# Quarter buffers at the in-projection's and the keys' operands; first quarters of each MLP loaded during the projection before it

## The chip, the cores and the metric

One Trainium2 chip, one core. The metric is the device time of one execution in microseconds (us); the kernel before was run three times, and the median counts. One further execution was taken by the hardware profiler, and all rows shown here come from it.

## The reference, cut to what matters

Batch 1, 512 tokens, width 1024, two layers, float32 throughout. Shown as code; `mlp` runs twice, once in each layer.

```python
def sq_relu_mlp(h, w1, w2):                 # w1 1024x4096, w2 4096x1024
    u = relu(h @ w1)
    return (u * u) @ w2

# layer 0: recurrent block
xb, yb = split(rmsnorm(x) @ w_in + b_in)            # in-projection, 1024x2048
hs = rg_lru(conv4(xb));  x = x + (hs * gelu(yb)) @ w_out   # out-projection, 1024x1024
x = x + sq_relu_mlp(rmsnorm(x), w1[0], w2[0])
k, v = split(rmsnorm(x) @ w_kv)
# layer 1: differential attention on k, v, 8 heads
x = x + diff_attention(rmsnorm(x) @ w_q, k, v) @ w_o       # attention's output projection
x = x + sq_relu_mlp(rmsnorm(x), w1[1], w2[1])
return rmsnorm(x)
```

## The kernel before, in words

Weights lie in memory as tiles of 128 x 1024 floats (512 KB) and are used in a fixed order. Each float32 tile is split into a high and a low part: ScalarE (ACT) copies it to `w_hi` (line 618), VectorE (DVE) subtracts to get `w_lo` (line 1120), and TensorE (PE) multiplies three times (hi by hi, hi by lo, lo by hi). `w_hi` and `w_lo` have four slots each, so the split of tile t waits until PE has done tile t-4. In the program's code "tile 20" is the fifth tile of the layer-0 out-projection: tiles 0 to 15 are the in-projection, 16 to 23 the out-projection, 24 to 51 the first of four groups of layer 0's MLP.

The MLP uses a seven-product scheme (Strassen's) on halves: each group of 1024 hidden units has seven products up and seven down, with two tiles of 24 matmuls for each product. Some products need sums of quarters of the weights. Those are built in two buffers, `q1` and `q2` (two tiles each). A plain load by the SyncE (SP) queue brings a quarter (A21, line 453), and GpSimd (POOL) issues an accumulating DMA that adds another quarter from memory onto it (line 547). A third step is an addition on DVE, `quarter_sum` (line 1452). The seven up products use, in order: A11 (ring), q2 = A21+A22, q2 plus A11 added by DVE, A12 (ring), q1 = A21+A11, q2 plus A12 added by DMA, A22 (ring).

Tiles that need no sum go through a ring of two raw buffers, `w_raw`, loaded by SP (line 442). Ring load r waits until the tile that used the buffer before is split. The two loads of A12 have one more condition: they wait for `quarter_sum`, since that reads A11 out of the ring buffers.

SP, ACT, DVE and POOL each run one program in order. For the first group of an MLP, SP's order is: all ring loads of the projection before; the two halves of q2; the two halves of q1; A11; A12; and on. These q loads wait for a semaphore that says the old data under the buffers is dead (`olo_done` for layer 0, `scores_mm` for layer 1). POOL's order is: `add_first` (A22 onto q2), the accumulation of the squares for the norm (`accumulate`, lines 535), then `add_others`, which begins with A11 onto q1.

`residual_step` runs on ACT and DVE beside the last projection tiles: for each of eight row blocks m it adds the projection to x, splits the weight tile four ahead, and builds the MLP's operands `x_raw`, `x_sum`, `x_hi`, `x_lo`. After it DVE does `quarter_sum` twice. In the first group, ACT and DVE then split tiles 4, 5, 6, 7 of the group (6 and 7 are A12), and only behind tile 7 compute the norm (`norm_guess`, `norm_newton`; its first DVE step is line 1170). PE starts the fourth up product only when the norm's sums have been copied out of a bank that this product uses (`sums_copied`). In layer 1 PE also transposes x between the first four products (`turn_x`, line 2001, eight blocks a pair); ACT empties the banks (`turned_rows`, line 905), in its program also behind the split of tile 7.

SBUF is shared over time: a region is used by the recurrent block, then by MLP 0; the attention uses the same addresses, then MLP 1. Before, `x_hi` and `x_lo` (28 KB a partition each) lie at the start and q1, q2 (8 KB each) behind them, over `lru_v` and `lru_x` in layer 0 and over `u_lo` and `kq` in layer 1. `in_hi` and `h_hi` are the first 16 KB.

Of the kernel before, what the change touches and what calls it, by code (L numbers as in the profile page):

```python
# [8 lines left out]
P = 128  # L9
D = 1024  # L10
S = 512
NCH = D // P
HEADS = 8
# [6 lines left out]
TILE = NCH * P  # L20
QB = S // P
# [14 lines left out]
T_OUT = len(IN_ORDER)  # L36
# [41 lines left out]
T_O = T_QK + 2 * HEADS  # L78
# [12 lines left out]
R_MLP0 = T_MLP0  # L91
R_V = R_MLP0 + R_PER * GROUPS
R_MLP1 = R_V + T_MLP1 - T_V
# [9 lines left out]
def up_tile(layer, g, p):  # L103
    return (T_MLP0, T_MLP1)[layer] + PER * g + p


def down_tile(layer, g, p):
    return up_tile(layer, g, 2 * NPROD + p)
# [19 lines left out]
A11, A12, A21, A22, B12, B11, B22, B21 = range(0, 16, 2)  # L128
# [4 lines left out]
def stored_tile(layer, g, place):  # L133
    return W_MLP[layer] + W_PER * g + place
# [7 lines left out]
O_M0 = O_Y + NCH  # L142
# [34 lines left out]
RING = 4  # L177
WARM_UP = 2
RAWS = 2
# [6 lines left out]
def build(nc, x_t, weights, gate_weights, vectors, lam_vecs, final_gain, out):  # L186
    F32 = mybir.dt.float32
# [5 lines left out]
    with keep:  # L193
        def sb(name, shape, dt, stack=keep):
            return stack.enter_context(nc.sbuf_tensor(name, shape, dt))

        def sem(name):
            return keep.enter_context(nc.semaphore(name))
# [7 lines left out]
        region = ExitStack()  # L206
# [12 lines left out]
        out_lo = sb("out_lo", [P, NCH, S], F32R, region)  # L219
        region.close()  # L220

        region = ExitStack()
        gain_rows = sb("gain_rows", [P, D], F32, region)
        region.close()

        region = ExitStack()
        x_hi = sb("x_hi", [P, NOP, PAIRS, HALF], F32R, region)
        x_lo = sb("x_lo", [P, NOP, PAIRS, HALF], F32R, region)
        q1 = sb("q1", [P, 2, TILE], F32, region)
        q2 = sb("q2", [P, 2, TILE], F32, region)  # L230
        first = ExitStack()
        x_raw0 = sb("x_raw0", [P, NCH, 2, HALF], F32, first)
        x_sum0 = sb("x_sum0", [P, 3, 4, HALF], F32, first)
# [69 lines left out]
        tile_done = sem("tile_done")  # L303
# [3 lines left out]
        olo_done = sem("olo_done")  # L307
# [34 lines left out]
        scores_mm = sem("scores_mm")  # L342
# [61 lines left out]
        def quarter_loads(layer, g, n):  # L404
            return 16 * (2 * (layer * GROUPS + g) + n + 1)
# [4 lines left out]
        def quarter_adds(layer, g, n, half):  # L410

            return 4 * (layer * GROUPS + g) + 2 * n + half + 1
# [8 lines left out]
        @block.sync  # L421
        def _(sp):
            def load_half(t, n):
                ks = slice(n * TILE // 2, (n + 1) * TILE // 2)
                sp.dma_start(w_raw[:, t, ks], weights[t][:, ks]).then_inc(half_in[2 * t + n], 16)

            def load_x(m):
                sp.dma_start(x[:, m, :], x_t[m]).then_inc(x_in[m], 16)


            load_x(0)
            load_half(0, 0)
            load_half(1, 0)
            load_x(1)
            load_half(0, 1)
            load_half(1, 1)
            for m in range(2, NCH):
                load_x(m)
            def load_ring(r, tile):

                sp.wait_ge(wlo_done, RING_TILES[r - RAWS] + 1)
                sp.dma_start(w_raw[:, r % RAWS, :], weights[tile]).then_inc(raw_in[r % RAWS], 16)

            def load_quarter(layer, g, q, place, free):

                for half in range(2):
                    if free is not None:
                        sp.wait_ge(wlo_done, free + half + 1)
                    elif layer:
                        sp.wait_ge(scores_mm, QB * HEADS)  # L450
                    else:
                        sp.wait_ge(olo_done, O_M0)
                    sp.dma_start(QUARTERS[q][:, half, :],
                                 weights[stored_tile(layer, g, place + half)]).then_inc(quarter_in[q][half], 16)

            def load_group(layer, g):
                r = (R_MLP0, R_MLP1)[layer] + R_PER * g

                def two(r, place):
                    for half in range(2):  # L460
                        load_ring(r + half, stored_tile(layer, g, place + half))

                load_quarter(layer, g, "q2", A21, down_tile(layer, g - 1, 8) if g else None)
                if g:
                    two(r, A11)
                    load_quarter(layer, g, "q1", A21, down_tile(layer, g - 1, 12))
                else:
                    load_quarter(layer, g, "q1", A21, None)
                    two(r, A11)
                for half in range(2):  # L470

                    sp.wait_ge(quarter_added, quarter_adds(layer, g, 0, half))
                    load_ring(r + 2 + half, stored_tile(layer, g, A12 + half))
                two(r + 4, A22)
                load_quarter(layer, g, "q1", B11, up_tile(layer, g, 8))
                load_quarter(layer, g, "q2", B12, up_tile(layer, g, 10))
                two(r + 6, B22)
                two(r + 8, B21)

            for r in range(RAWS, R_MLP0):  # L480
                load_ring(r, r)
            for g in range(GROUPS):
                load_group(0, g)
            for r in range(R_V, R_MLP1):
                load_ring(r, W_MLP[1] - R_MLP1 + r)
            for g in range(GROUPS):
                load_group(1, g)


            sp.wait_ge(tile_done, down_tile(1, GROUPS - 1, 0))  # L490
            sp.dma_start(gain_rows[:, :], final_gain).then_inc(gain_in, 16)

            for n, tok in enumerate((0, 1, 2, 3)):
                for half, done in ((1, out_act), (0, out_dve)):
                    sp.wait_ge(done, n + 1)
                    sp.dma_start(out[tok][:, HALVES[half]], y[:, tok, HALVES[half]]).then_inc(stored, 16)
            sp.wait_ge(stored, 16 * QB * 2)
# [3 lines left out]
        def _(pool):  # L501
# [36 lines left out]
            def add_quarter(layer, g, q, place, split=None, loaded=None, added=None):  # L538

                for half in range(2):  # L540
                    if loaded is not None:
                        pool.wait_ge(quarter_in[q][half], quarter_loads(layer, g, loaded))
                    if split is not None:
                        pool.wait_ge(wlo_done, split + half + 1)
                    if added is not None:
                        pool.wait_ge(quarter_added, quarter_adds(layer, g, added, half))
                    nc.gpsimd.dma_start(QUARTERS[q][:, half, :], weights[stored_tile(layer, g, place + half)],  # L547
                                        accum_op=ALU.add).then_inc(sum_in[q][half], 16)

            def add_first(layer, g):  # L550
                add_quarter(layer, g, "q2", A22, loaded=0)

            def add_others(layer, g):
                add_quarter(layer, g, "q1", A11, loaded=0)
                add_quarter(layer, g, "q2", A12, split=up_tile(layer, g, 4))
                add_quarter(layer, g, "q1", B22, split=down_tile(layer, g, 2))
                add_quarter(layer, g, "q2", B22, loaded=1, added=1)
                add_quarter(layer, g, "q1", B21, split=down_tile(layer, g, 4))

            add_first(0, 0)  # L560
            accumulate(N_M0, 0)
            def constants():
# [12 lines left out]
                                        ALU.add).then_inc(consts_done, 1)  # L575

            add_others(0, 0)
            constants()
            for g in range(1, GROUPS):
                add_first(0, g)  # L580
                add_others(0, g)

            add_first(1, 0)
            accumulate(N_M1, 1)
            add_others(1, 0)
            for g in range(1, GROUPS):
                add_first(1, g)
# [519 lines left out]
        def _(dve):  # L1107
            own = Own(dve, dve_own)

            def split_lo(t):  # L1110
                if t >= TILES:
                    return
                quarter = quarter_of(t)
                if quarter is None:
                    src = w_raw[:, RING_OF[t] % RAWS, :]
                else:
                    _, _, (q, _, _, _), half = quarter
                    src = QUARTERS[q][:, half, :]
                dve.wait_ge(whi_done, t + 1)
                nc.vector.tensor_tensor(w_lo[:, t % RING, :], src, w_hi[:, t % RING, :],  # L1120
                                        ALU.subtract).then_inc(wlo_done, 1)
# [1210 lines left out]
```

## Time and profile before

| | us |
|---|---|
| three runs | 1055.74, 1056.50, 1056.93 |
| median | 1056.5 |
| profiled execution, its own time | 1058.89 |
| its span in the profile | 1057.1 |
| PE busy in the span | 1035.2 (98%) |
| DVE busy | 813.7 (77%) |
| ACT busy | 644.7 (61%) |
| mean granted TensorE clock | 0.994 |

Busy times are of one engine each; they run beside each other. The span is from the first to the last instruction that the profile shows. A granted clock of 1.00 is 2.4 GHz and 0.50 is 1.2 GHz.

### The profile page before, as it was taken

Reading aid. Unit: us, or ns where it says so; the run is one execution under the profiler, and the core shown is the slowest. Engines: PE = TensorE matmul, PEld = TensorE weight load, DVE = VectorE, ACT = ScalarE, POOL = GpSimd, SP = SyncE. Lnnn points to the kernel's source line nnn. Section 1 sums busy time; section 2 is a strip of 40 time slices with the busy share of each in tenths; the row PEclk is TensorE's granted clock in tenths of the full one; section 3 lists DMA queues with packets and bytes.
Section 4 is the critical chain, followed back from the end, with each engine's and each line's share of the span. In section 5 each row is a group of like instructions: output and inputs, shape, how many; then the busy total and the mean of one; then the engine's idle time right before and its main releaser. Section 6 shows DMA issues by size and latency. Waiting matters only on the chain.

```text
span 1057.1 us, 15296 instructions
## 1 busy us (share of the span) xinstructions
PE 1035.2 (98%) x5920; PEld 885.5 (84%) x5920; DVE 813.7 (77%) x1157; ACT 644.7 (61%) x940; POOL 108.2 (10%) x133
## 2 busy tenths in 40 slices
PE   8999999999999999999999999999899999999995
PEld 6777889979989989988877777779888988988984
DVE  6988875886896896898656666566598698698697
ACT  7698864745745745665336656566664664664665
POOL 1000021121111101100000000012011011011012
PEclk9999999999999999999999999999999999999998
DMA  7222288498498498462321111167779678779672
GB/s 253 91 81 80 81 229 211 117 252 231 115 256 228 118 258 230 115 173 88 112 63 58 60 60 41 60 187 145 207 143 246 209 151 244 203 152 252 193 156 104
DMA packets 47592, 165.29 MB, mean 156 GB/s; under 512 B 5408, under 2 KB 5536, under 8 KB 47392
## 3 DMA queue, kind: packets, MB, share of 16 engines
q1 hardware_dynamic: 31536, 109.59, 30.2%
q0 software_dynamic: 15552, 53.48, 27.7%
q10 hardware_dynamic: 432, 1.24, 0.3%
q8 instruction: 47, 0.77, 0.3%
q14 instruction: 25, 0.20, 0.1%
HBM read 159.05 MB, written 2.10 MB: 152 GB/s over the span
## 4 chain that ended last, share of the span: by engine, by line
PE 87%; DVE 5%; DMA 5%; ACT 1%; issue 1%; SPq 0%; DVEq 0%; ACTq 0%
PE ps L1982 27%; PE ps L2017 27%; PE ps L1849 21%; DMA w_raw<-weights 5%; PE ps L2080 4%; PE ps L2139 2%; PE ps L2165 2%; DVE w_lo L1120 1%; PE ps L1908 1%; PE ps L2154 1%; DVE value L1499 1%; ACT w_hi L618 1%; DVE acc L1149 0%; DVE q L1452 0%; DVE x_lo L1401 0%
## 5 line engine op out<-in xcount | busy, mean ns | idle before, releaser
L1982 PE MATMUL ps<-x_hi,w_hi 128*128 128x256 f32 x896 | 255.2, 285 | 3.3 <-DVE cols L1170 2.0
L1982 PE MATMUL ps<-x_lo,w_hi 128*128 128x256 f32 x896 | 254.4, 284 | 0.0
L1982 PE MATMUL ps<-x_hi,w_lo 128*128 128x256 f32 x896 | 254.3, 284 | 0.0
L618 ACT ACTIVATE w_hi<-w_raw 128x1024 fp32r<-128x1024 f32 x134 | 140.5, 1055 | 170.2 <-DMA w_raw<-weights 127.8
L1120 DVE TENSOR_TENSOR w_lo<-w_raw,w_hi 128x1024 fp32r<-128x1024 f32 x134 | 163.9, 1224 | 89.4 <-ACT w_hi L618 88.9
L1120 DVE TENSOR_TENSOR w_lo<-q,w_hi 128x1024 fp32r<-128x1024 f32 x144 | 176.3, 1227 | 42.9 <-ACT w_hi L618 42.0
L618 ACT ACTIVATE w_hi<-q 128x1024 fp32r<-128x1024 f32 x144 | 150.9, 1052 | 93.4 <-PE ps L1982 42.1
L2017 PE MATMUL ps<-w_hi,a_hi 128*128 128x512 f32 x448 | 176.2, 393 | 1.8 <-DVE w_lo L1120 1.2
L1982 PEld LDWEIGHTS ps<-x_hi,w_hi 128*128 128x128 f32 x896 | 172.9, 193 | 4.1 <-DVE cols L1170 2.2
L2017 PE MATMUL ps<-w_hi,a_lo 128*128 128x512 f32 x448 | 174.6, 390 | 0.0
L2017 PE MATMUL ps<-w_lo,a_hi 128*128 128x512 f32 x448 | 174.5, 390 | 0.0
L547 POOL DMA_DIRECT2D q<-weights x96 | 83.5, 965 | 882.7 <-DMA q<-weights 515.8
L1982 PEld LDWEIGHTS ps<-x_lo,w_hi 128*128 128x128 f32 x896 | 173.0, 193 | 0.3
L1982 PEld LDWEIGHTS ps<-x_hi,w_lo 128*128 128x128 f32 x896 | 172.9, 193 | 0.0
L2017 PEld LDWEIGHTS ps<-w_hi,a_hi 128*128 128x128 f32 x448 | 84.1, 188 | 25.1 <-issue 4.6
L2017 PEld LDWEIGHTS ps<-w_lo,a_hi 128*128 128x128 f32 x448 | 84.1, 188 | 17.9
L2017 PEld LDWEIGHTS ps<-w_hi,a_lo 128*128 128x128 f32 x448 | 84.2, 188 | 16.3
L1499 DVE SCALAR_TENSOR_TENSOR value<-ps,scale,value 128x512 f32<-128x512 f32 x104 | 73.0, 742 | 3.2 <-PE ps L2017 2.8
L1849 PE MATMUL ps<-in_hi,w_hi 128*128 128x512 f32 x128 | 54.3, 424 | 1.8 <-DVE in_lo L1125 0.8
L1849 PE MATMUL ps<-in_lo,w_hi 128*128 128x512 f32 x128 | 50.5, 395 | 0.0
L1849 PE MATMUL ps<-in_hi,w_lo 128*128 128x512 f32 x128 | 50.4, 394 | 0.0
L976 ACT ACTIVATE prob_t<-ps 128x512 f32<-128x512 f32 (+3 forms) x32 | 14.1, 441 | 44.1 <-PE ps L2165 23.7
(218 smaller groups left out, 1666.8 us busy)
## 6 DMA issues: line engine op xcount, KB each, us to landing
w_raw<-weights SPq DMA_DIRECT2D x134, 512.0 KB, 4.4
q<-weights POOLq DMA_DIRECT2D x96, 512.0 KB, 8.1
q<-weights SPq DMA_DIRECT2D x64, 512.0 KB, 4.6
x<-x_t SPq DMA_DIRECT2D x8, 256.0 KB, 6.6
y_t<-value SPq DMA_DIRECT2D x8, 256.0 KB, 2.3
acc<-work POOLq DMA_DIRECT2D x6, 256.0 KB, 3.3
rstd<-work POOLq DMA_DIRECT2D x6, 256.0 KB, 3.5
w_raw<-weights SPq DMA_DIRECT2D x4, 256.0 KB, 4.7
```

The costliest lines, as they stand in the source:

```text
L547: nc.gpsimd.dma_start(QUARTERS[q][:, half, :], weights[stored_tile(layer, g, place + half)], accum_op=ALU.add).then_inc(sum_in[q][half], 16)
L618: nc.scalar.activation(w_hi[:, t % RING, :], src, ACT.Copy).then_inc(whi_done, 1)
L976: nc.scalar.activation(prob_t[:, j % 2, 0:n], ps[:, BANK_T, 0:n], ACT.Copy).then_inc(trans_read, 1)
L1120: nc.vector.tensor_tensor(w_lo[:, t % RING, :], src, w_hi[:, t % RING, :], ALU.subtract).then_inc(wlo_done, 1)
L1499: return nc.vector.scalar_tensor_tensor(out=to, in0=bank, scalar=scale2[:, half, tok:tok + 1], in1=to, op0=ALU.mult, op1=ALU.add)
L1849: ins = nc.tensor.matmul(ps[:, bank, :], w[:, slot, ws], o[:, k, :], start=(k == 0 and n == 0), stop=(k == NCH - 1 and n == 2))
L1908: ins = nc.tensor.matmul(ps[:, bank, :], gw[:, ws], lru_v[:, m, :], start=True, stop=True)
L1982: ins = nc.tensor.matmul(to, w[:, t % RING, ws], o[:, op, j, :], start=fresh and j == 0 and f % 2 == 0 and n == 0, stop=j == PAIRS - 1 and ...
L2017: ins = nc.tensor.matmul(ps[:, bank, :], a[:, a_slot, j, ts], w[:, slot, ws], start=first and a is a_hi and w is w_hi, stop=end and w is w ...
L2080: ins = nc.tensor.matmul(ps[:, 4 * half + tok, :], o[:, k, ts], w[:, t % RING, cs], start=(i == 0 and n == 0), stop=(i == NCH - 1 and n == 2))
L2139: ins = nc.tensor.matmul(ps[:, BANK_SCORES + 2 * (j % 2) + c, 0:n], kq[rows, h % 2, 1, qb * P:(qb + 1) * P], kq[rows, h % 2, 0, 0:n], star ...
L2165: ins = nc.tensor.matmul(ps[:, BANK_O, qb * P:(qb + 1) * P], prob_t[:, j % 2, kb * P:(kb + 1) * P], value[:, kb, h * P:(h + 1) * P], start ...
```

## The change

The two quarter buffers move to the first 16 KB of the region, that is over `in_hi` (in-projection operand) and over `h_hi` (the keys' operand); `x_hi` and `x_lo` move 16 KB up. Their first loads wait for the end of the in-projection (`tile_done` 16) and of the last key tile (`tile_done` T_O). On SP these four loads move ahead of three ring loads in layer 0's out-projection (right behind ring load 20) and ahead of two ring loads in layer 1's output projection (behind ring load R_MLP1-3). On POOL the addition of A11 onto q1 moves from `add_others` to `add_first`, ahead of the accumulation of squares. Groups 1 to 3 keep their orders.

```diff
+        q1 = sb("q1", [P, 2, TILE], F32, region)
+        q2 = sb("q2", [P, 2, TILE], F32, region)
+        final = ExitStack()
+        gain_rows = sb("gain_rows", [P, D], F32, final)
+        final.close()
         x_hi = sb("x_hi", [P, NOP, PAIRS, HALF], F32R, region)
         x_lo = sb("x_lo", [P, NOP, PAIRS, HALF], F32R, region)
-        q1 = sb("q1", [P, 2, TILE], F32, region)
-        q2 = sb("q2", [P, 2, TILE], F32, region)
...
                     if free is not None:
                         sp.wait_ge(wlo_done, free + half + 1)
-                    elif layer:
-                        sp.wait_ge(scores_mm, QB * HEADS)
                     else:
-                        sp.wait_ge(olo_done, O_M0)
+                        sp.wait_ge(tile_done, (T_OUT, T_O)[layer])
...
-                load_quarter(layer, g, "q2", A21, down_tile(layer, g - 1, 8) if g else None)
                 if g:
-                    two(r, A11)
+                    load_quarter(layer, g, "q2", A21, down_tile(layer, g - 1, 8))
+                two(r, A11)
+                if g:
                     load_quarter(layer, g, "q1", A21, down_tile(layer, g - 1, 12))
-                else:
-                    load_quarter(layer, g, "q1", A21, None)
-                    two(r, A11)
...
+            def first_quarters(layer):
+                load_quarter(layer, 0, "q2", A21, None)
+                load_quarter(layer, 0, "q1", A21, None)
+
             for r in range(RAWS, R_MLP0):
                 load_ring(r, r)
+                if r == R_MLP0 - RING:
+                    first_quarters(0)
...
             for r in range(R_V, R_MLP1):
                 load_ring(r, W_MLP[1] - R_MLP1 + r)
+                if r == R_MLP1 - RAWS - 1:
+                    first_quarters(1)
...
             def add_first(layer, g):
                 add_quarter(layer, g, "q2", A22, loaded=0)
+                add_quarter(layer, g, "q1", A11, loaded=0)
 
             def add_others(layer, g):
-                add_quarter(layer, g, "q1", A11, loaded=0)
```

## Rows read from the trace of the kernel before

**Rows 1.** Waits of PE over the whole span: us in total, times, longest.
```profile
PE ps L2001 <- ACT value L905: 3.2, 1, 3.2
PE ps L1982 <- DVE cols L1170: 2.0, 1, 2.0
PE ps L1982 <- DVE x_lo L1401: 1.3, 1, 1.3
```
**Rows 2.** Stretches; after the engines' busy us come granted clock, DMA share, GB/s.
```profile
177.00:178.00 1.00, 1.00 (x6) 1.00 (x6) 0.99 (x3) 1.00 (x2) 0.00 (x0) 0.50 1.03 274
...
724.00:726.00 2.00, 2.00 (x18) 2.00 (x19) 1.21 (x3) 1.48 (x3) 0.67 (x1) 1.00 0.43 76
...
744.00:745.00 1.00, 0.80 (x4) 0.80 (x5) 0.86 (x4) 1.00 (x3) 0.00 (x0) 0.50 1.02 270
```
**Rows 3.** The chain that ended last, in order of time: start, us, what.
```profile
163.18 10.73 DMA w_raw<-weights
...
176.37 24.79 PE ps L1982 x192
...
397.66 40.31 PE ps L1982 x336
...
731.63 10.56 DMA w_raw<-weights
...
752.32 0.87 PE ps L2001 x8
753.19 17.27 PE ps L1982 x144
```
**Rows 4.** PE in order of time: where stages begin, and before the longest gap.
```profile
111.59 0.39 PE L1849 MATMUL ps<-out_hi,w_hi 128*128 128x512 f32 x1
...
155.11 0.28 PE L1982 MATMUL ps<-x_hi,w_hi 128*128 128x256 f32 x1
...
718.14 0.28 PE L1982 MATMUL ps<-x_hi,w_hi 128*128 128x256 f32 x1
...
740.71 0.28 PE L1982 MATMUL ps<-x_hi,w_lo 128*128 128x256 f32 x1
```
**Rows 5.** POOL, ACT and DVE in order of time, 160 to 176 us.
```profile
160.68 2.12 POOL L547 DMA_DIRECT2D q<-weights  x2
...
173.93 1.06 ACT L618 ACTIVATE w_hi<-w_raw 128x1024 fp32r<-128x1024 f32 x1 [2.93 <-DMA w_raw<-weights]
...
175.02 1.22 DVE L1120 TENSOR_TENSOR w_lo<-w_raw,w_hi 128x1024 fp32r<-128x1024 f32 x1 [3.68 <-ACT w_hi L618]
```
**Rows 6.** The page's queues (packets, MB, share of 16 engines), q1 SP's, q0 POOL's.
```profile
q1 hardware_dynamic: 31536, 109.59, 30.2%
q0 software_dynamic: 15552, 53.48, 27.7%
```
**Rows 7.** From issue to landing, DMAs of `w_raw`, then of `q`.
```profile
DMA to landing us min/median/max: 3.2/4.4/10.7
DMA to landing us min/median/max: 3.4/6.9/13.3
```
**Rows 8.** SP's issues of the first quarters, layer 0 and layer 1.
```profile
131.39 1.88 SPq L453 DMA_DIRECT2D q<-weights  x4
...
699.12 1.86 SPq L453 DMA_DIRECT2D q<-weights  x4
```
**Rows 9.** DVE: splits of tile 18, of tile 21, and of layer 1's tile T_O+3.
```profile
109.45 1.22 DVE L1120 TENSOR_TENSOR w_lo<-w_raw,w_hi 128x1024 fp32r<-128x1024 f32 x1
...
129.76 1.23 DVE L1120 TENSOR_TENSOR w_lo<-w_raw,w_hi 128x1024 fp32r<-128x1024 f32 x1
...
679.38 1.22 DVE L1120 TENSOR_TENSOR w_lo<-w_raw,w_hi 128x1024 fp32r<-128x1024 f32 x1
```
**Rows 10.** Stretches of four us, columns as in rows 2.
```profile
120.00:124.00 4.00, 4.00 (x19) 3.34 (x18) 3.04 (x5) 2.31 (x4) 0.00 (x0) 1.00 0.00 2
...
684.00:688.00 4.00, 4.00 (x23) 3.34 (x22) 0.65 (x4) 2.06 (x13) 0.00 (x0) 1.00 0.01 4
```

More of the change, by code:

```diff
@@ L222, in build @@
         region = ExitStack()
-        gain_rows = sb("gain_rows", [P, D], F32, region)
-        region.close()
-        region = ExitStack()
+        q1 = sb("q1", [P, 2, TILE], F32, region)
[3 more added lines that the diff above has]
+        final.close()
         x_hi = sb("x_hi", [P, NOP, PAIRS, HALF], F32R, region)
         x_lo = sb("x_lo", [P, NOP, PAIRS, HALF], F32R, region)
-        q1 = sb("q1", [P, 2, TILE], F32, region)
-        q2 = sb("q2", [P, 2, TILE], F32, region)
         first = ExitStack()
```

## The prediction

> **What bounds the kernel now.** I read the table of busy times first: PE is busy 1035.2 of 1057.1 us, so only PE's gaps, and stretches in which its clock is low, can be won by moving transfers. Then PE's waits, to see which gaps there are. Three of the largest lie where an MLP begins: 2.0 us before the fourth up product of layer 0, and in layer 1 1.3 and 3.2 us [rows 1]. The windows then show the clock: 0.50 at 177 us and at 744 us, after each of the two longer gaps, but 1.00 after the gap of 1.3 us [rows 2]. Last the chain, to see what made the gaps: in both layers it runs through one ring load, the second half of A12, that takes 10.7 and 10.6 us [rows 3], where the median of all ring loads is 4.4 [rows 7].
>
> The named releasers are not the cause. In layer 0 the wait is put down to the norm's first step on DVE, but by program order that step stands behind the split of tile 7 (A12's second half), which ACT begins at 173.93 after 2.9 us of waiting for the DMA, and DVE ends at 176.24 [rows 5]. In layer 1 the emptying of the transposes' banks stands behind the same split. The DMA is slow because of company: POOL has put two accumulating transfers (A11 onto q1) in flight at 160.68 [rows 5], and two more follow.
>
> **What the gaps cost in all.** A 256-column matmul costs 40.31/336 = 0.120 us in steady state [rows 3].
> - Layer 0: PE restarts at 176.37 after 2.05 idle, so it was free at 174.3. The 192 matmuls from there take 24.79 where 192 x 0.120 = 23.04 would do [rows 3]: 1.75 us of half clock. Together 3.8 us.
> - Layer 1, long gap: PE is free at 740.71 + 0.28 = 740.99 [rows 4], and the fifth product starts at 753.19 [rows 3]. Between lie two groups of eight transposes (0.87 us each [rows 3]) and 48 matmuls (5.76): 7.5 us of work in 12.2 us. Loss 4.7 us.
> - Layer 1, short gap: 1.3 us [rows 1].
>
> Sum 9.8 us: that is the most this change can take out of these places.
>
> **The change part by part.**
>
> *Loads of the first quarters earlier.* Four loads a layer. Nothing is added; queue shares give their price: SP's queue moves 109.59 MB in 30.2% of 1057.1 us, so 512 KB (0.524 MB) occupy all 16 engines for 1.53 us; POOL's accumulating queue 53.48 MB in 27.7%, so one accumulating transfer 2.87 us [rows 6]. Layer 0: ring load 20 is issued when tile 18 is split (110.7 [rows 9]); the wait for the in-projection ends at about 111.6 to 112, when out_hi matmuls have begun [rows 4]. The loads then go out some 19.5 us before their present 131.4 [rows 8]. Layer 1: ring load T_O+5 goes out when T_O+3 is split, 680.6 [rows 9]; the last key tile was done before, so the wait is met, and the loads are issued at 681 instead of 699.1 [rows 8]. Both stretches have idle DMA: share 0.00 at 120 to 124 and 0.01 at 684 to 688 [rows 10].
>
> *Both additions right behind them.* 4 x 1.53 + 4 x 2.87 = 17.6 us of DMA a layer. Layer 0: from 112, over by about 131 if little else is served. Layer 1: 681 to 699, so it is out of the way when the last splits begin. POOL has nothing ahead of these issues that is pending and nothing behind that is due earlier (the squares come from ACT at about 135), so its queue loses nothing. Issue costs (0.47 us on SP, about 0.9 on POOL) lie on idle queues.
>
> *The new wait on SP.* Behind it are ring loads 21 to 23, of which 21 may not be issued before tile 19 is split, at 124.5. The wait ends 12 us before that: cost 0. The same in layer 1, with T_O+6 at about 696.
>
> *Ring loads delayed in layer 0.* Load 21 (124.5) now meets the rest of the additions: up to (131 - 124.5) = 6.5 us of DMA work, or none. Tile 21's split ended at 131.0 [rows 9]; PE needs it 16.32 us (three tiles of 5.44) before 155.11, at 138.8 [rows 4]. So 7.8 us of cover against at most 6.5: cost 0, or up to 1 us with no cover left. From 131 on the ring loads meet less than before.
>
> *A12 loads, layer 0.* Their issue is fixed by quarter_sum: the second at 163.18, which is 8.07 after the first up matmul at 155.11 [rows 3, 4]. Two additions less in flight are 5.7 us less of DMA work. Before, it landed at 173.9; now at 173.9 - 5.7 = 168.2. With 1.06 and 1.22 for the splits the norm starts at 170.6, against PE's need at 174.3: gap 0, 3.7 us to spare. Bounds: if the load gets none of the 5.7 us, the gap of 2.0 and the slow clock stay (3.8 us kept); if all, 0. I take 0, since the engines were saturated at that time (DMA share 1.03 right after [rows 2]).
>
> The Trainium skill ("DMA: Bandwidth & Descriptors", the anatomy of one SWDGE transfer) gives about 2.0 us plus bytes / 436 GB/s for any such transfer, so by it (an estimate) the two additions carry only 2.4 us, A12 lands at 171.5, the norm starts at 173.9 and PE still waits for nothing, with 0.4 us to spare. The queue shares of this trace give 2.87 us for each [rows 6], more than twice the rule; I go by the trace.
>
> *Layer 1.* The 1.3 us gap is x_lo of row block 6, whose DVE steps sit behind splits that waited for A11's late ring load. With q loads and additions over by 699 this load is alone with its kind (3.2 to 4.4 us [rows 7]), and the residual steps follow PE as in layer 0, where this gap does not exist: 1.3 won. Second A12 load: 718.14 + 8.07 = 726.2 instead of 731.6 [rows 3, 4]. It takes 10.56 - 5.74 = 4.8, lands at 731.0; ACT is through tile 7, the norm and the two bank copies at about 733.7. PE arrives at 740.99 - 1.3 = 739.7: gap 0, 6 us to spare, 4.7 won. If the load kept its full 10.6 us it would land at 736.8 and still be in time: layer 1's gain does not hang on the DMA's price.
>
> *Addresses.* x_hi and x_lo lie 16 KB higher. A steady up phase mixes reads of both, which lie 28 KB apart, and comes out at an even 0.120 a matmul [rows 3]; no row shows another placement. I take 0; the third digit of that mean bounds it, 0.0005 x 2688 matmuls = 1.3 us either way.
>
> *What is late next.* Tiles 8 and 9 (q1) are ready early; tiles 10 and 11 need A12 onto q2, issued at 164.8 and 166.7 as before but with less company, and PE wants them at 174.3 + 11.5 = 185.8. From there on the groups are PE-bound: the middle groups take 40.31 us up with no gap. The kernel's tail hangs on PE's end and shifts with it.
>
> Sum: 3.8 + 1.3 + 4.7 = 9.8 us. The profiled execution took 1058.89 (span 1057.1); 9.8 less gives 1049.1 (span 1047.3). The runs' median, 1056.5, is 2.4 below the profiled one; the same difference gives **1046.7**.
>
> **The rivals.**
> 1. *Layer 0 keeps its gap in part.* For it: only 3.7 us of reserve, and load 21 to 25 now mix with additions, so DVE might reach quarter_sum later. Against: the reserve above. If nothing is won there: 1056.5 - 6.0 = 1050.5; if 0.5 us of gap stays without a drop of the clock, as after the 1.3 us gap [rows 2]: 1047.2.
> 2. *The change doesn't reach the gaps.* The norm itself is late (squares by accumulating DMA) and not the split ahead of it. For it: the named releaser. Against: PE ran its sums for the norm during the second product without waiting. Time 1056.5.
> 3. *Slower.* Place: layer 0's out-projection. The early transfers lengthen ring loads 21 to 25. Two buffers give a loop: two tiles per load time + 2.3 us for the splits, while PE uses two in 10.9, so it falls behind when a load takes over 8.6 us, and 7.8 us are in hand. At the longest landing seen, 13.3 [rows 7], 2.5 pairs lose 11.8, less 7.8, plus 1.75 for the clock: 5.7 us, time 1052.4. It decides the sign from loads of 15.0 us on; at twice the longest ring load (21.4) it costs 26 and gives 1072.7. The Trainium skill (same page, "Issuing engines are not separate DMA queues") says that transfers of all queues interleave on the same 16 engines, which is this mechanism; the slow A12 loads agree with it. Against: only 17.6 us of DMA work in all, most of it over before load 21.
>
> **How the numbers follow.** Forecast 0.74 (1045.8 to 1047.8). Rival 1: 0.18 (1047.2 to 1050.5). Rival 2: 0.03. Rival 3: 0.05, of which 0.03 ends slower. The range has the forecast and rival 1 in it, and 1.4 us below the forecast for addresses and for small DMA waits that also go: 1045.3 to 1050.5. A measurement tells 0.2% (2.1 us) from no change; faster 0.94, same 0.03, slower 0.03.
>
> **What would show it.** PE's waits for DVE cols, ACT value and DVE x_lo gone; clock 1.00 through both starts; the A12 loads at 4 to 6 us; first fourth-product matmul of layer 0 at 174.3; q additions at 113 to 131 and 682 to 699; PE busy in layer 0's out-projection. It is wrong if A12 still takes over 8 us, if PE waits in the out-projection, or if the first groups get new gaps.

## The result, and the profile after

The changed kernel takes 1047.52 us in the median of four runs (1046.32 to 1047.70), the one before 1056.55 (1055.74 to 1056.93). The ratio is 0.9913 with a 95% interval of 0.9896 to 0.9930, so 7.4 to 11.0 us less. In a later comparison with more rounds the same kernel had 1047.39 against 1057.03, ratio 0.9904 (0.9890 to 0.9918). The prediction was 1046.7 in a range of 1045.3 to 1050.5.

Two rival explanations stood against the forecast's ("company": A12's loads are slow because the two additions of A11 are in flight beside them) when the experiments began: that the new addresses make the gain ("layout"), and that the early loads do it by themselves ("earliness").

First PE's waits in the profile after (us in total, times, longest). None of the three waits of [rows 1] is left: none for the banks' copies, for the norm's first step or for x_lo.

```profile
PE ps L1919 <- POOL cols L513: 1.7, 1, 1.7
PE ps L2022 <- DVE w_lo L1125: 1.3, 1, 1.3
PE ps L1854 <- DVE w_lo L1143: 0.7, 1, 0.7
PE ps L1854 <- DVE w_lo L1125: 0.4, 1, 0.4
```

All four were there before too (1.7, 1.2, 0.7 and 0.4 us). The chain that ended last (start, us, what) shows both starts as PE alone; in [rows 3] it ran through ring loads of 10.7 and 10.6 us. The first five lines are layer 0, the rest layer 1.

```profile
99.91 54.40 PE ps L1854 x240
154.31 11.51 PE ps L1987 x96
165.82 1.68 PE ps L1897 x16
167.50 28.90 PE ps L1987 x240
196.40 8.64 PE ps L2022 x38
...
720.10 5.75 PE ps L1987 x48
725.85 1.68 PE ps L1897 x16
727.53 0.93 PE ps L2006 x8
728.46 5.75 PE ps L1987 x48
734.21 0.87 PE ps L2006 x8
735.08 5.75 PE ps L1987 x48
740.83 0.87 PE ps L2006 x8
741.71 17.27 PE ps L1987 x144
```

Windows of the profile after, columns as in [rows 2]; first one where [rows 2] had half clock, then four us of layer 1's up matmuls. PE is busy throughout at full clock, and in the first the DMA moves 90 GB/s.

```profile
177.00:178.00 1.00, 1.00 (x11) 1.00 (x9) 0.55 (x1) 0.42 (x1) 0.00 (x0) 1.00 0.74 90
...
728.00:732.00 4.00, 4.00 (x36) 4.00 (x35) 2.09 (x8) 2.85 (x6) 0.00 (x0) 1.00 1.02 215
```

The page's queues after: as many packets and bytes as in [rows 6], so the change moved transfers and took none away.

```profile
q1 hardware_dynamic: 31536, 109.59, 30.3%
q0 software_dynamic: 15552, 53.48, 28.0%
```

SP and POOL in order of time in the profile after. The four loads a layer go out at 110.8 and 676.2, where [rows 8] had 131.4 and 699.1, and all four additions follow at once.

```profile
110.82 1.77 SPq L452 DMA_DIRECT2D q<-weights  x4
...
676.17 1.86 SPq L452 DMA_DIRECT2D q<-weights  x4
```

```profile
115.73 1.03 POOL L552 DMA_DIRECT2D q<-weights  x1 [109.34 <-DMA q<-weights]
...
120.46 0.86 POOL L552 DMA_DIRECT2D q<-weights  x1 [0.47 <-DMA q<-weights]
...
680.73 0.84 POOL L552 DMA_DIRECT2D q<-weights  x1 [232.84 <-DMA q<-weights]
...
685.97 0.86 POOL L552 DMA_DIRECT2D q<-weights  x1 [1.35 <-DMA q<-weights]
```

ACT and DVE in layer 0 after: the late split of tile 21 (the price of the early transfers), and A12's second half with the norm behind it. In [rows 5] ACT began that split at 173.93, after 2.93 us of waiting for the DMA; now it begins at 166.78 and waits for nothing, for the load landed at 166.60, 4.4 us after its issue, where it had taken 10.7.

```profile
132.07 1.06 ACT L623 ACTIVATE w_hi<-w_raw 128x1024 fp32r<-128x1024 f32 x1 [4.26 <-DMA w_raw<-weights]
133.16 1.23 DVE L1125 TENSOR_TENSOR w_lo<-w_raw,w_hi 128x1024 fp32r<-128x1024 f32 x1 [4.42 <-ACT w_hi L623]
...
166.78 1.05 ACT L623 ACTIVATE w_hi<-w_raw 128x1024 fp32r<-128x1024 f32 x1
...
169.00 0.15 DVE L1175 TENSOR_SCALAR cols<-ps 128x4 f32<-128x4 f32 x1
```

Layer 1's long gap has one cause more. There A12's loads themselves went out late, since `quarter_sum` waits for A11's ring loads. The second of these took 10.5 us before (the chain, first line below); after, ACT begins the splits of both halves of A11 (the other two lines) without a wait.

```profile
705.75 10.49 DMA w_raw<-weights
```

```profile
703.63 1.04 ACT L623 ACTIVATE w_hi<-w_raw 128x1024 fp32r<-128x1024 f32 x1
...
707.08 1.04 ACT L623 ACTIVATE w_hi<-w_raw 128x1024 fp32r<-128x1024 f32 x1
```

Counted from the first up matmul of layer 1, the second load of A12 went out at 13.5 us before and at 9.7 after.

Two stretches tell the rest, and they can be read from every profile: from the first up matmul of an MLP to its first down matmul. "Start" is when PE begins layer 0's MLP, "rest" what follows layer 1's stretch. The labels are explained with the experiments.

| profile | start | layer 0 | between | layer 1 | rest | span |
|---|---|---|---|---|---|---|
| before | 155.11 | 45.89 | 517.14 | 52.16 | 286.80 | 1057.1 |
| before, second profile | 154.41 | 45.61 | 517.87 | 51.40 | 287.41 | 1056.7 |
| layout only | 154.94 | 44.10 | 517.40 | 50.05 | 287.21 | 1053.7 |
| layer 0 only | 154.09 | 42.10 | 517.14 | 50.90 | 286.07 | 1050.3 |
| layer 1 only | 154.40 | 44.01 | 517.90 | 45.49 | 287.10 | 1048.9 |
| loads early, additions late | 154.58 | 45.62 | 517.66 | 45.69 | 287.15 | 1050.7 |
| loads late, additions early | 154.75 | 42.09 | 517.63 | 53.66 | 285.07 | 1053.2 |
| plain loads for additions | 154.83 | 42.57 | 517.31 | 48.54 | 285.95 | 1049.2 |
| company put back | 154.87 | 44.10 | 517.89 | 45.50 | 285.94 | 1048.3 |
| each layer its own half | 154.74 | 42.09 | 518.11 | 45.63 | 286.53 | 1047.1 |
| loads later | 155.40 | 42.09 | 517.77 | 51.66 | 285.58 | 1052.5 |
| after | 154.15 | 42.09 | 517.07 | 45.50 | 286.89 | 1045.7 |
| after, second profile | 154.09 | 42.09 | 517.99 | 45.50 | 286.33 | 1046.0 |

Before to after: 0.96 at the start (the first DMAs, which the change does not touch), 3.80 in layer 0, 6.66 in layer 1, 0.07 and -0.09 elsewhere; 11.4 in all. The start and the rest move by up to 1.3 and 2.3 us between executions, with nothing changed there: layer 0's out-projection, into which the early transfers were moved, takes 43.52 us in all thirteen profiles. So the difference of one profiled pair of spans is not the gain; the two stretches show it.

### The profile page after: what moved, and what is told of

It is laid out like the page before. It is cut to its first block, busy times and chain, and to the rows that moved or that the text cites. A ratio compares the mean times of both kernels' runs of the same rounds, so it can differ in the third digit from the quotient of the medians.

```text
span 1045.7 us, 15296 instructions
## 1 busy us (share of the span) xinstructions
PE 1031.0 (99%) x5920; PEld 882.9 (84%) x5920; DVE 813.3 (78%) x1157; ACT 645.5 (62%) x940; POOL 107.4 (10%) x133
## 4 chain that ended last, share of the span: by engine, by line
PE 91%; DVE 4%; DMA 2%; issue 1%; ACT 1%; SPq 0%; POOL 0%; DVEq 0%; ACTq 0%; POOLq 0%
PE ps L1987 30%; PE ps L2022 26%; PE ps L1854 23%; PE ps L2085 4%; PE ps L2144 2%; PE ps L2170 2%; PE ps L1913 1%; DVE w_lo L1125 1%; DMA w_raw<-weights 1%; PE ps L2159 1%; DVE value L1504 1%; DMA q<-weights 1%; ACT w_hi L623 1%; DVE acc L1154 0%; DMA x<-x_t 0%
## 5 line engine op out<-in xcount | busy, mean ns | idle before, releaser
L981 ACT ACTIVATE prob_t<-ps 128x512 f32<-128x512 f32 (+3 forms) x32 | 14.1, 440 | 44.1 <-PE ps L2170 23.7
```

The source lines that it names most:

```text
L981: nc.scalar.activation(prob_t[:, j % 2, 0:n], ps[:, BANK_T, 0:n], ACT.Copy).then_inc(trans_read, 1)
```

## The experiments

**The kernel before, profiled again** (no edit).

> The kernel before, unchanged, profiled a second time. The two profiled spans differ by 11.4 us (1057.1 to 1045.7) while the medians differ by 9.0. If the first profiled execution was slow by chance, this one has a span near 1054.7 (median less 1.8) with the layer-0 start about 1 us earlier and the gaps at both MLP starts a little smaller; if it is the profiler, the span is again about 1057. Either way ratio 1.000, and the same three gaps (2.0, 1.3, 3.2 us) within some tenths.

Measured: 1056.38 against 1056.51 us, ratio 0.9999 (0.9986 to 1.0012), span 1056.7. Two gaps are there, 1.8 and 3.3 us; the x_lo gap is only 0.2 where [rows 1] had 1.3. The start is 0.7 us earlier. The span is the "again about 1057" of the expectation and not the 1054.7 that chance would have given. But a constant price of profiling isn't shown either: both profiled executions of this kernel lie 2.2 to 2.4 us above the median of its runs, those of the other kernels between 1.8 us below theirs and 1.7 above. Why these two were slow stays open. A12's second half takes 10.45 and 10.64 us, as before.

**Layout only.** Both layers' first quarters at the old places in SP's and POOL's order; new addresses and the new semaphore stay.

```diff
+                if not g and layer in (0, 1):
+                    load_quarter(layer, g, "q2", A21, None)
+                    load_quarter(layer, g, "q1", A21, None)
                 if g:
...
                 if r == R_MLP0 - RING:
-                    first_quarters(0)
+                    pass
...
                 if r == R_MLP1 - RAWS - 1:
-                    first_quarters(1)
+                    pass
...
             def add_first(layer, g):
                 add_quarter(layer, g, "q2", A22, loaded=0)
-                add_quarter(layer, g, "q1", A11, loaded=0)
+                if g or layer not in (0, 1):
+                    add_quarter(layer, g, "q1", A11, loaded=0)
 
             def add_others(layer, g):
+                if not g and layer in (0, 1):
+                    add_quarter(layer, g, "q1", A11, loaded=0)
```

> Only the addresses of q1, q2, x_hi and x_lo and the semaphore the first loads wait for are new; loads and additions are issued at the old places. Company theory: 1056.5 (ratio 1.000), all three gaps there. Layout theory: part of the gain, or a loss, appears here: more than 1 us either way.

Measured: 1056.76 against 1056.51, ratio 1.0002 (0.9989 to 1.0014). Layout falls. The gaps are there (1.8, 0.5 and 1.7 us), the last half as long as in the two profiles of before. PE came to it later: the granted clock was 0.50 from 731.9 to 735.3 us, before this gap and not after it, with no wait of PE over 0.1 us since the one of 0.5 at 721.4.

**One layer at a time.** The same edits for one layer only, the other as in the whole change.

> New layout, early loads and both early additions in layer 0 only; layer 1's first quarters loaded and added at the old places. If the gain is the sum of two independent starts: 3.8 us (layer 0's part of the 9.8) less what the first profiled run overstated, so 1052.6 to 1053.5; layer 1 keeps its gaps of 1.3 and 3.2 us. If the layout alone gives the gain: 1047.5. If only one layer counts: 1047.5 or 1056.5.

> The counterpart: layer 1 only. Independent starts: 6.0 us, so 1050.5 to 1051.5, layer 0 keeps a gap of 2.0 us and half clock behind it. Together with the run with layer 0 alone the gains should add up to the 9.0 of the whole change within 0.5.

Measured: layer 0 only 1053.89 against 1056.51, ratio 0.9977 (0.9968 to 0.9986); layer 1 only 1050.86, ratio 0.9950 (0.9937 to 0.9963). "Layer 0 only" is 0.4 us slower than its expected range, "layer 1 only" lies in its own. The gains are 2.6 and 5.7 us, 8.3 together, against 9.0 and 9.6 for the whole change: the intervals overlap, but the sum is not within the 0.5 that was expected. In the profiles each layer has its own stretch repaired (42.10 and 45.49), and the other keeps its gap (1.7 us in layer 0, 3.1 in layer 1), so the starts are independent.

**Loads early, additions late.**

```diff
             def add_first(layer, g):
                 add_quarter(layer, g, "q2", A22, loaded=0)
-                add_quarter(layer, g, "q1", A11, loaded=0)
+                if g or layer not in (0, 1):
+                    add_quarter(layer, g, "q1", A11, loaded=0)
 
             def add_others(layer, g):
+                if not g and layer in (0, 1):
+                    add_quarter(layer, g, "q1", A11, loaded=0)
```

> After, but GpSimd issues A11 onto q1 at the old place, behind the accumulation of squares, in both layers; the loads stay early. Company theory: the two additions are again in flight beside A12, so layer 0's gap comes back (A12 takes about 10.7 us, loss 3.8 us), in layer 1 the A12 load is again about 10 us but starts 5.4 us earlier and lands at about 726 + 10 = 736, before PE needs it, so layer 1 keeps its 6.0: 1050.5 to 1051.5. Theory that the early loads are what counts: 1047.5.

Measured: 1050.86 against 1055.82, ratio 0.9952 (0.9935 to 0.9969). As the company theory said: layer 0 has its gap (1.8 us) with half clock behind it and gains nothing (45.62), layer 1 has its whole gain (45.69); its A12 was split at 736.7, where 736 was expected, in time for PE. Earliness falls for layer 0 and stands for layer 1.

**Loads late, additions early.** The edit to SP's order from "layout only", POOL's order from the change.

> New layout, loads at the old places, but A11 onto q1 is issued right behind A22 onto q2. Company theory: A12 has no company in either layer (4 to 6 us), but four additions and four loads crowd the last projection tiles: A11's ring loads land later than before (layer 0: 3 to 5 us later than 147, so the split of tile 25 at about 152 and the residual steps late). Layer 0 may lose 0 to 3 us from that, layer 1's 1.3 us gap grows to 3 to 6 us, its 3.2 us gap shrinks or goes: 1050 to 1056. Theory that additions alone count: 1047.5.

Measured: 1056.17 against 1055.82, ratio 1.0001 (0.9986 to 1.0016). Layer 0 loses nothing by the crowd and has its whole gain (42.09). Layer 1 loses 1.5 to 2.3 us against before (53.66), but not by the gap that I expected. The longest gap is a new one. POOL's issues, PE's longest wait and the chain in that profile:

```profile
704.58 1.20 POOL L543 DMA_DIRECT2D acc<-work  x1
705.12 1.55 POOL L543 DMA_DIRECT2D rstd<-work  x1
720.27 0.86 POOL L543 DMA_DIRECT2D acc<-work  x1 [13.61 <-ACT work L637]
```

```profile
731.79 0.35 PE L1900 MATMUL ps<-ones,acc 128*128 128x1 f32 x2 [4.27 <-DMA rstd<-work]
```

```profile
704.58 14.46 DMA acc<-work
...
720.90 4.22 DMA rstd<-work
...
725.65 6.01 DMA rstd<-work
```

A 256 KB accumulation of squares takes 14.5 us beside four loads and four additions; before, beside four loads and two additions, it had taken 12.4. ACT may not overwrite its buffer before it lands, so the later squares come late. The last of them meets A12's loads too and takes 6.0 us, and PE's sums for the norm wait 4.3 us for it, after which the granted clock is 0.50 until 739.6. The squares' own DMAs were the cost that I had not priced.

**Each layer its own half.** Layer 0 with early additions and late loads, layer 1 with early loads and late additions.

> New layout; layer 0 gets only the early additions (its loads stay at the old place), layer 1 only the early loads (its A11 additions stay at the old place). The profiles of the two half changes had layer 0's start at 42.1 us with additions early alone (46 before), and layer 1's start at 45.7 with loads early alone (52 before), against 42.1 and 45.5 in the whole change. If each layer needs just that half: the time of the whole change within 1 us, start stretches of 42.1 and 45.7. If the halves need each other: 3 to 4 us slower than the whole change.

Measured: 1047.26 against 1057.03, ratio 0.9903 (0.9890 to 0.9917), where the whole change in the same comparison has 0.9904. The halves don't need each other: early additions in layer 0 and early loads in layer 1 give all of the gain.

**The whole change again** (no edit).

> The whole change, unchanged, on the same chip as the two others and with more rounds: 1047 to 1048, ratio 0.991 to 0.992; start stretches 42.1 and 45.5 us and no clock drop. It gives the ratio that the halves are compared with.

Measured: 1047.39, ratio 0.9904 (0.9890 to 0.9918), stretches 42.09 and 45.50.

**Loads later.**

```diff
-                if r == R_MLP0 - RING:
+                if r == R_MLP0 - RING + 2:
                     first_quarters(0)
...
-                if r == R_MLP1 - RAWS - 1:
+                if r == R_MLP1 - RAWS:
                     first_quarters(1)
```

> After, but the first quarters are loaded two ring loads later in layer 0 and one later in layer 1, 2 to 3 us ahead of the old places instead of 20 and 18. Theory that freeing the stretch before the last splits is what helps layer 1: its four loads, four additions and the squares' accumulating transfers meet the A11 loads as in the run with early additions alone, the norm's sums wait for the squares again, and layer 1's start takes 49 to 53 us instead of 45.5; layer 0 stays at 42.1. Time 1050 to 1055. Theory that the order on GpSimd alone matters: the time of the whole change.

Measured: 1052.61 against 1057.03, ratio 0.9953 (0.9936 to 0.9970). Layer 0 keeps its gain (42.09), layer 1 has 51.66, within the 49 to 53 that were expected. But PE doesn't wait for the squares here. The crowd strikes the ring loads: the chain goes through the load of T_O+7 and A11's, PE waits 3.35 us for x_lo, and the granted clock is 0.50 from then until 728.7.

```profile
695.85 8.28 DMA w_raw<-weights
...
706.50 8.92 DMA w_raw<-weights
```

```profile
723.08 0.58 PE L1987 MATMUL ps<-x_hi,w_hi 128*128 128x256 f32 x1 [3.35 <-DVE x_lo L1406]
```

**Company put back.** The whole change, with two accumulating transfers into dead memory (x_raw1) in layer 0; the two plain loads that prepare this memory are issued by SP at the MLP's start, before A12's are in flight.

```diff
...
+            def company():
+                for half in range(2):
+                    pool.wait_ge(scratch_in[half], 16)
+                    nc.gpsimd.dma_start(x_raw1[:, 2 * half:2 * half + 2, :, :].rearrange("p m n s -> p (m n s)"),
+                                        weights[stored_tile(0, 0, A11 + half)],
+                                        accum_op=ALU.add).then_inc(company_in, 16)
...
+            company()
             add_others(0, 0)
```

> After, with two accumulating transfers of 512 KB into dead memory put back in layer 0 at the place where A11's additions stood before (two plain loads prepare that memory at 154 to 159 us, when the DMA is idle). Nothing else is moved. Company theory: A12's second half takes 10 to 11 us again instead of 4.5, PE waits 1.5 to 2.5 us and runs 3 us at half clock: loss 3.3 to 4.0 us, 1050.8 to 1051.5. If earliness or layout made the gain: 1047.5.

Measured: 1051.48 against 1055.82, ratio 0.9954 (0.9935 to 0.9972). The preparing loads land at 158.8 and 160.0, the first load of A12 goes out at 161.8, so they are not its company. In this profile the chain has A12's second half again, 10.4 us as before, and PE's gap is 1.8 us.

```profile
162.94 10.44 DMA w_raw<-weights
```

The profiled execution lost only 2.0 us by it (44.10 against 42.09), since the clock did not fall; the ratio is 0.0041 to 0.0050 above those of the whole change, 4.3 to 5.3 us. That is more than layer 0's stretch ever lost (3.8), but each ratio is uncertain by 0.002, some 2 us, and they come from different comparisons.

**Plain loads for additions.** The kernel before; in the first group of each MLP the two additions of A11 are plain loads.

```diff
+                    if g == 0 and q == "q1" and place == A11:
+                        nc.gpsimd.dma_start(QUARTERS[q][:, half, :],
+                                            weights[stored_tile(layer, g, place + half)]).then_inc(sum_in[q][half], 16)
+                        continue
```

> The kernel before with the first group's A11 onto q1 (two transfers a layer) as plain loads in place of accumulating ones, which leaves A21 out of that sum. Prices from the queue shares (2.87 us an addition, 1.53 us a plain load): 2.7 us less of DMA work beside A12, which lands about 2.7 us earlier: gap of layer 0 gone (2.0 us and its clock), 3.2 us gap of layer 1 down to about 0.5 to 1: gain 6 to 7.5 us, 1049 to 1050.5. If an addition costs the DMA engines no more than a plain load: 1056.5, A12 at 10.7 us.

Measured: 1051.72 against 1055.82, ratio 0.9963 (0.9949 to 0.9977), 2.4 to 5.4 us: less than the 6 to 7.5 expected. (The kernel leaves A21 out of a sum; its times alone are of use.) The load of A12's second half in layer 0:

```profile
162.90 8.90 DMA w_raw<-weights
```

8.9 us instead of 10.45, and 8.8 instead of 10.6 in layer 1. So two additions cost A12 1.6 to 1.8 us more than two plain loads do, where the queue shares promised 2.7. It was enough for layer 0 (gap 0.2, stretch 42.57); layer 1 kept gaps of 0.7 (x_lo), 0.5 (squares) and 1.1 us.

## Why the prediction was right

*The gaps and their cause.* Right. The part of the sum that lies in layer 0 is the company of the two additions: without them 42.1 us, with them or with stand-ins for them 44 to 46, whatever else is early or late (plain loads in their place: 42.6). A12's second half was forecast to land 13.1 us after the MLP's start (168.2 - 155.1); it landed after 12.5. Its load became 6.3 us shorter (10.73 to 4.39) where the price of two additions was put at 5.7. The time alone wouldn't tell: 1047.5 lies in the forecast's 1045.8 to 1047.8, but also in the 1047.2 to 1050.5 of rival 1. That PE has no gap left in either start decides it.

*Layer 0's term, 3.8 us.* The same in the first pair of profiles (45.89 to 42.09), but its 1.75 us of half clock are no constant. Six profiles have a gap of 1.7 to 2.0 us at this place; in three the clock fell (before, before again, additions late: 45.6 to 45.9), in three it did not (layout only, layer 1 only, company put back: 44.0 to 44.1). Windows of one us in the layout-only profile, then in the second profile of before; the clock is the third number from the end.

```profile
175.00:176.00 1.00, 0.09 (x1) 0.09 (x1) 0.90 (x3) 1.00 (x2) 0.00 (x0) 1.00 1.05 279
176.00:177.00 1.00, 1.00 (x9) 1.00 (x10) 0.90 (x6) 1.00 (x2) 0.00 (x0) 1.00 1.05 279
177.00:178.00 1.00, 1.00 (x11) 1.00 (x10) 1.00 (x2) 0.73 (x1) 0.00 (x0) 1.00 1.02 274
```

```profile
174.00:175.00 1.00, 0.00 (x0) 0.00 (x0) 0.95 (x1) 0.97 (x4) 0.00 (x0) 1.00 1.01 238
...
177.00:178.00 1.00, 1.00 (x7) 1.00 (x6) 1.00 (x2) 0.21 (x1) 0.00 (x0) 0.50 0.99 348
178.00:179.00 1.00, 1.00 (x7) 1.00 (x7) 0.54 (x1) 0.00 (x0) 0.00 (x0) 0.50 1.19 410
```

Where the clock stayed, the stretch is 1.9 to 2.0 us longer than without a gap; where it fell, 3.5 to 3.8. The half clock is worth about 1.5 us of that, in three profiles of six. Taken over these profiles the term is 1.9 to 3.8 us; "layer 0 only" gained 2.6 in the medians. This is the term that was mis-sized, on one profile.

*Layer 1's term, 6.0 us.* A little small: 6.66 and 5.90 in the two pairs. In the first pair the long gap with its half clock took the 4.7 us of the sum; the short gap took 1.6, with the slow restart behind it, where 1.3 stood, and the stretch from the norm's sums to the transposes was 0.3 longer before. The ring loads were as prompt as forecast: A11's took 3.4 and 3.6 us (7.0 and 10.5 before), A12's second 4.9 (4.8 forecast). It went out 9.7 us after the MLP's start, where I had 8.07. I wrote that the gain did not hang on the price of the additions, which holds (additions late: 45.69, A11's loads 3.6 and 3.5 us, A12's second out at 8.1). What it does hang on I left unsaid: when the quarters' loads go out. In the six profiles in which they do so some 37 us ahead of layer 1's MLP, its stretch is 45.5 to 45.7. At 21.6 us ahead, only 2.5 before the old place, it is 51.66, and additions moved without the loads make it worse (53.66). No run lies between. In layer 0 the old place was 23.7 us ahead of the MLP, in layer 1 only 19.0; that this is why layer 0 doesn't need its loads early is likely, but no run shows it.

*Edits costed at nothing.* The addresses: right within the interval (ratio 1.0002, 0.9989 to 1.0014). The wait on SP: right, the loads went out at 110.8 and 676.2. Ring load 21 was given up to 6.5 us of delay against 7.8 of cover. Its split ended at 134.4, 19.8 us before the MLP's start against 24.1 before: 4.4 us later, with 3.4 left.

*The rivals.* Rival 3 (the crowd falls behind) is real as a mechanism, and did not decide in the place named for it: layer 0's stretch was 42.09 however late the loads went out, as long as the additions were early. It decides in layer 1, when the loads come late, and there through the squares as well as through the ring. Rival 1 and rival 2 did not occur. The Trainium skill's rule for the price of a transfer ("DMA: Bandwidth & Descriptors", the section on the anatomy of one DMA on the SWDGE path) makes an addition as cheap as a load; the runs put it between that and the queue shares: an addition is 0.8 to 0.9 us dearer to the load beside it than a plain load, where the shares gave 1.34.

*The sum.* 9.8 us against 9.0 and 9.6 in the medians of two comparisons. It was read from one profiled execution that was 2.4 us slower than the median and had half clock behind both long gaps, and was taken off the median whole. In the first pair of profiles the two stretches gave 10.5.

## What to carry to other kernels

A wait that is put down to a small instruction can belong to a DMA that an instruction ahead of it in program order waited for; look at what else is in flight then, and move that. Moving transfers early paid here where they went out in an idle stretch, well ahead of the next stage's own transfers; a few us ahead of the old place gave only half the gain, and layer 1's additions without its loads cost all that layer 0 had won. And a clock loss behind a gap of 2 us, seen once, is not to be counted on: here it came in three profiles of six.

## What the runs showed of the hardware that was not expected

The granted clock after a gap of TensorE of 1.7 to 2.0 us fell to 0.50 in three of six profiles and stayed at 1.00 in three, at the same place of nearly the same program; after 3.1 to 4.3 us (layer 1, in five profiles: both of before, layer 0 only, loads later, loads late with additions early) it fell each time. In the layout-only profile it also fell at 731.9 us without a wait of PE over 0.1 us in the 10 us before, and stayed at 1.00 behind the gap of 1.7 us at 741.6. An accumulating 256 KB transfer within SBUF took 14.5 us beside four loads and four additions of 512 KB (12.4 beside four loads and two additions), against a median of 3.3 in the kernel before. And the device time of the unchanged kernel ran from 1053.1 to 1060.9 us in the 26 executions of one comparison; in the thirteen profiles the start and what follows layer 1's stretch, which no edit touches, move by up to 1.3 and 2.3 us, about as much as the smaller part of this change is worth.
